# Where the seven-product partial sums are gathered, and how many blocks are dense, in a float32 transformer layer on one core

## The reference

```python
def swiglu(x, w_gate, w_up, w_down):
    return (jax.nn.silu(x @ w_gate) * (x @ w_up)) @ w_down

def reference(...):                      # DEPTH = 1, D_MODEL = 2048, FFN_DIM = 5632
    h = swiglu(rms_norm(x, ffn1_pre_g[l]), ffn1_w_gate[l], ffn1_w_up[l], ffn1_w_down[l])
    x = x + 0.5 * rms_norm(h, ffn1_post_g[l])
    ...                                  # attention part, untouched
    h = swiglu(rms_norm(x, ffn2_pre_g[l]), ffn2_w_gate[l], ffn2_w_up[l], ffn2_w_down[l])
    x = x + 0.5 * rms_norm(h, ffn2_post_g[l])
```

## Time and profile before

| | |
|---|---|
| time, median of 3 runs | 1757.99 us (1757.85 to 1758.72) |
| span of the profiled execution | 1756.5 us (the page has no separate time for it) |
| TensorE busy | 1737.1 us, 99% |
| VectorE busy | 1410.7 us, 80% |
| ScalarE busy | 1001.8 us, 57% |
| DMA | 389.75 MB, mean 222 GB/s |

### The profile page before, as it was taken

One profiled execution on the slowest core, in us unless ns is written; L12 is line 12 of the kernel. 1 busy time (PEld: TensorE's weight loads), 2 busy tenths in 40 slices (PEclk: granted clock), 3 DMA queues, 4 the chain that ended last, 5 costly groups with the idle time before them and its releaser, 6 DMA issues. The chain is left out here.

```text
span 1756.5 us, 21394 instructions
## 1 busy us (share of the span) xinstructions
PE 1737.1 (99%) x7968; PEld 1442.3 (82%) x7968; DVE 1410.7 (80%) x1284; ACT 1001.8 (57%) x979; POOL 65.3 (4%) x99
## 2 busy tenths in 40 slices
PE   9999999999999999999999999999999999999998
PEld 8788888888888888788888878788888888888886
DVE  7888888888888888765578558888888888888887
ACT  6666565555655654543347446555666666555563
POOL 1000000000000000010000000000000000000000
PEclk9999999999999999999999999999999999999999
DMA  9777777777766554355441546777777777666453
GB/s 386 237 257 259 256 256 239 239 239 248 245 234 222 184 215 176 147 219 189 174 162 54 187 171 260 263 240 241 249 249 241 239 246 251 254 232 238 174 191 114
DMA packets 58978, 389.75 MB, mean 222 GB/s; under 512 B 6432, under 2 KB 6688, under 8 KB 16160
## 3 DMA queue, kind: packets, MB, share of 16 engines
q1 hardware_dynamic: 52720, 344.77, 50.1%
q0 software_dynamic: 6048, 44.04, 13.2%
q10 hardware_dynamic: 144, 0.04, 0.0%
HBM read 384.63 MB, written 4.19 MB: 221 GB/s over the span
## 5 line engine op out<-in xcount | busy, mean ns | idle before, releaser
L2093 PE MATMUL banks<-w_hi,act_hi 128*128 128x512 f32 (+1 forms) x1088 | 424.7, 390 | 1.1 <-DVE act_lo L1355 1.1
L2095 PE MATMUL banks<-w_hi,act_lo 128*128 128x512 f32 (+1 forms) x1088 | 421.5, 387 | 0.0
L2094 PE MATMUL banks<-w_lo,act_hi 128*128 128x512 f32 (+1 forms) x1088 | 421.2, 387 | 0.0
L1385 DVE TENSOR_TENSOR op_lo<-quads,op_hi 128x2048 fp32r<-128x2048 f32 x140 | 318.5, 2288 | 43.2 <-ACT op_hi L918 42.8
L918 ACT ACTIVATE op_hi<-quads 128x2048 fp32r<-128x2048 f32 x140 | 266.8, 1919 | 53.3 <-PE banks L2095 21.1
L2287 PE MATMUL banks<-w_hi,hid_split 128*128 128x512 f32 x992 | 275.1, 389 | 0.5 <-DVE hid_split L1616 0.5
L1374 DVE TENSOR_TENSOR w_lo<-raw,w_hi 128x2048 fp32r<-128x2048 f32 x80 | 181.3, 2287 | 78.3 <-ACT w_hi L892 78.3
L1344 DVE TENSOR_TENSOR w_lo<-raw,w_hi 128x2048 fp32r<-128x2048 f32 (+3 forms) x67 | 143.8, 2147 | 121.6 <-ACT w_hi L843 121.6
L2093 PEld LDWEIGHTS banks<-w_hi,act_hi 128*128 128x128 f32 x1088 | 204.6, 188 | 42.1 <-issue 1.8
L2095 PEld LDWEIGHTS banks<-w_hi,act_lo 128*128 128x128 f32 x1088 | 204.4, 188 | 41.7
L2094 PEld LDWEIGHTS banks<-w_lo,act_hi 128*128 128x128 f32 x1088 | 204.6, 188 | 40.0
(11 more groups left out here) (209 smaller groups left out, 2329.8 us busy)
## 6 DMA issues: line engine op xcount, KB each, us to landing
raw<-in_weights SPq DMA_DIRECT2D x203, 1024.0 KB, 5.1
quads<-in_paired SPq DMA_DIRECT2D x80, 1024.0 KB, 10.7
quads<-in_paired POOLq DMA_DIRECT2D x40, 1024.0 KB, 8.5
raw<-in_paired SPq DMA_DIRECT2D x32, 768.0 KB, 5.9
rows<-in_x SPq DMA_DIRECT2D x4, 1024.0 KB, 10.9
raw<-in_weights SPq DMA_DIRECT2D x6, 512.0 KB, 3.5
gain_row<-in_post_gains SPq DMA_DIRECT2D x3, 1024.0 KB, 6.6
raw<-in_weights SPq DMA_DIRECT2D x4, 768.0 KB, 4.1
```

Source lines behind the costliest of these rows:

```text
L1385: nc.vector.tensor_tensor(op_lo[:, slot, :], op_raw(op), op_hi[slot][:, :], ALU.subtract)\
L2093: nc.tensor.matmul(out_ap, hi, rhs_hi, start=start, stop=False, skip_group_check=chain)
L2094: nc.tensor.matmul(out_ap, hi, rhs_lo, start=False, stop=False, skip_group_check=chain)
L2095: return nc.tensor.matmul(out_ap, lo, rhs_hi, start=False, stop=stop, skip_group_check=chain)
```

## The change

- `DENSE = 4`: blocks 0 to 3 are dense, so that nine units are left. Blocks 0 to 2 run ahead of the first unit. Block 3 runs inside it: its four pieces (`ahead`, B_0 to B_3) stand where a unit has plain pieces, and a unit's own plain pieces follow one unit later, except one. TensorE's order in a unit is P3, P1, L_A, P7, P6, turn, L_B, P2, L_C, P5, P4, turn, L_D. L_D holds near chunks of this unit; L_A (near), L_B and L_C (far) are those of the unit before. After the last unit L_A, L_B, L_C remain as a tail.
- The gathering moves into PSUM. ScalarE copies P3 and P7 to SBUF and P1 into the near block's bank, each times the inverse of the RMS factor (`inv`); VectorE begins the three other banks with `inv` times X plus or minus a kept part (`begin_bank`). The remaining products and the plain pieces then accumulate on these banks. SiLU and the product with the up half read them, with the RMS factor as scale. `join_part` and `mix_block` go.
- The near block's banks alternate (2, 3 and 6, 7); the far block's are 0, 1.
- P1's activations get their own scaled copy (`a11_hi`, `a11_lo`); `act_hi` keeps its values.
- The two accumulating DMAs are cut in rows of 1024 elements instead of 2048.
- The SP queue's loads follow the new order; the second unit's L_A waits for `piece_used` of B_3.
- In the down stage's start the order of the first pieces changes a little.

```diff
-UNITS = N_FB // 2
+DENSE = 4
+UNITS = (N_FB - DENSE) // 2
...
-            def join_part(part, t, other, op=ALU.add):
-                nc.vector.tensor_tensor(part[:, t, :], part[:, t, :], other, op).then_inc(parts_joined, 1)
-
-            def mix_block(stage, u, part, bank, behind, joined, sign=ALU.add):
...
+            def begin_bank(bank, t, negative, kept_part, op):
+                nc.vector.scalar_tensor_tensor(
+                    out=banks[:, bank, :], in0=banks[:, X_BANK, :], scalar=inv[:, negative, t:t + 1], in1=kept_part,
+                    op0=ALU.mult, op1=op).then_inc(banks_added, 1)
+            def begin_near(stage, v):
+                dve.wait_ge(part_kept, per_unit(stage, v.u, 3, 3))
+                dve.wait_ge(piece_used, used(stage, v, O_P6))
+                begin_bank(near_bank(v) + 1, 1, 0, kept7[:, :], ALU.add)
+            def begin_far(stage, v):
...
+                dve.wait_ge(piece_used, used(stage, v, O_P5))
+                begin_bank(FAR_BANK, 0, 1, kept3[:, :], ALU.add)
+                begin_bank(FAR_BANK + 1, 1, 1, kept7[:, :], ALU.subtract)
```

ScalarE's kept and begun parts, and its unit:

```diff
+            def keep_p3(stage, v):
...
+                nc.scalar.activation(kept3[:, :], banks[:, near_bank(v), :], ACT.Copy, scale=inv[:, 0, 0:1])\
+                  .then_inc(part_kept, 1)
+            def begin_near(stage, v):
...
+                nc.scalar.activation(banks[:, near_bank(v), :], banks[:, X_BANK, :], ACT.Copy, scale=inv[:, 0, 0:1])\
+                  .then_inc(part_kept, 1)
+            def keep_p7(stage, v):
...
+            def unit(stage, v, last=False):
+                keep_p3(stage, v)
+                operand_high(stage, v, O_P7)
+                begin_near(stage, v)
+                operand_high(stage, v, O_P6)
+                plain_high(stage, v, L_B)
+                gate_near(stage, before, v)
+                plain_high(stage, v, L_C)
+                keep_p7(stage, v)
+                operand_high(stage, v, O_P2)
                 operand_high(stage, v, O_P5)
+                keep_hidden(stage, near_block(before))
+                plain_high(stage, v, L_D)
                 operand_high(stage, v, O_P4)
+                gate_far(stage, before, v)
+                plain_high(stage, behind, L_A)
+                if not last:
+                    operand_high(stage, behind, O_P3, v)
+                    operand_high(stage, behind, O_P1, v)
+                keep_hidden(stage, far_block(before))
```

VectorE's unit:

```diff
             def unit(stage, v, last=False):
+                sum2(stage, v)
                 operand_low(stage, v, O_P7)
                 operand_low(stage, v, O_P6)
+                plain_low(stage, v, L_B)
+                multiply_hidden(stage, near_block(before), near_bank(before))
+                plain_low(stage, v, L_C)
                 operand_low(stage, v, O_P2)
+                begin_near(stage, v)
+                operand_low(stage, v, O_P5)
+                plain_low(stage, v, L_D)
                 operand_low(stage, v, O_P4)
+                multiply_hidden(stage, far_block(before), FAR_BANK)
+                plain_low(stage, behind, L_A)
+                begin_far(stage, v)
                 if not last:
+                    operand_low(stage, behind, O_P3)
+                    operand_low(stage, behind, O_P1)
+                    sum3(stage, behind)
```

TensorE's first unit, and from the SP and POOL queues the wait for B_3 and the size of an accumulating load's rows:

```diff
+            def first_unit(stage):
+                v = FIRST
                 product(stage, v, O_P3)
                 product(stage, v, O_P1)
+                turn_hidden(stage, 2)
+                ahead_product(stage, 0)
                 product(stage, v, O_P7)
                 product(stage, v, O_P6)
+                ahead_product(stage, 1)
+                product(stage, v, O_P2)
+                ahead_product(stage, 2)
                 product(stage, v, O_P5)
+                ahead_product(stage, 3)
+                product(stage, v, O_P4)
+                plain_product(stage, v, L_D, v)
...
+                    sp.wait_ge(piece_used, used(stage, v, B_3))
+                    load_plain(stage, behind, L_A)
...
                                     .rearrange("o p n -> (o p) n"), accum_op=ALU.add,
+                                    max_dma_last_dim=2 * OPERAND).then_inc(sum1_landed, 16)
```

More of the change, by code:

```diff
@@ L646, in load_units @@
[L646 to L651 removed]
+                sp.wait_ge(lo_ready, made(stage, LAST, L_B))
+                load_plain(stage, LAST, L_D)
+                sp.wait_ge(lo_ready, made(stage, LAST, L_C))
```

714 lines of the change are left out of this document (401 added, 313 removed).

## The result

The changed kernel takes 1761.84 us (median of 20 runs, 1759.69 to 1766.48), the kernel before, run beside it, 1758.68 us (20 runs, 1757.59 to 1759.95). The ratio is 1.0021, 95% interval [1.0014, 1.0027]: about 3 us and just over 0.2% slower, where I had forecast 1758.2 us and no difference. It lies inside the stated range (1756.0 to 1763.5) and 0.3 us above the 0.2% band. Its runs also spread more, 6.8 us against 2.4.

What follows compares the result with a forecast made beforehand. TensorE, busy 1737.1 of 1756.5 us, bounds the kernel. Span 1756.5 + 5.4 (products) - 6.0 (waits) + 0.8 (second unit's P1) = 1756.7, with 1.5 us over the span 1758.2 us; range 1756.0 to 1763.5.

Steps and rivals of the forecast that it cites:

- 0.2% band: Whole kernel: 0.2% or 3.5 us is about what a measurement can tell from no change, 1754.5 to 1761.5 us.
- the side that I had given 0.22: Whole kernel: slower than before by more than 0.2%, chance 0.22.
- other rivals: Range's upper end 1763.5: waits returning elsewhere (0.13), middle-unit cover used up (0.06), late second-unit L_A and P1 (0.18).
- 24 matmuls, +5.4 us: Gate/up stages: two dense blocks more, one unit less per network add 12 matmuls each, +5.4 us on TensorE.
- The waits of the old first units, -6.0 us: Start of both gate/up stages: TensorE's waits and late steps, 3.0 us per network, all go.
- Middle units unchanged: Middle gate/up units: they keep 41.77 us without TensorE waits; less helper work gives nothing there.
- P1 of the second unit, +0.8 us: Second unit: L_A, requested only when B_3 is used, makes P1 0.4 us late, twice; really late: chance 0.18.
- Second accumulating load: Each unit, ahead of P4: issued at 10.3, landed by 20 us; even with doubled landing in time, no cost.
- The down stage ... No change.: Start of the down stage: VectorE has the first piece ready 1 us before, so no added time.
- The clock: Idle time at 1044 to 1046 us: drop cost about 1.7 us; spared 1755.7, chance 0.06; striking twice 1759.9.
- the third: First units: old waits return at other places, half of the 6.0 us stay, 1761.2 us; chance 0.13.

Runs made afterwards that it cites:

- combined version: Changed kernel with accumulating loads in long rows, side sums moved before the last block's second plain piece, pauses filled with products of zeros: 1757.55 us, ratio 0.9992.
- room experiment: Changed kernel, short rows kept, with 1792 instead of 1024 bytes per partition set aside for GpSimd's transfer descriptions: 1760.42 us, ratio 1.0006.
- run with held loads: Changed kernel with SyncE's loads behind the second unit's near-block third piece held until that unit's second accumulating load has landed: 1768.93 us, ratio 1.0053.

## Where the prediction was right, and where it failed

The time lies inside the range, but 3.6 us above the forecast, on the side that I had given 0.22. The mechanism that I built the forecast on held: the added products and the removed waits nearly cancel, and nothing happens in the middle units. What made the kernel slower came from terms that I had put at nothing, the second accumulating load above all. The range had room for them only because I had widened it for other rivals; that the time fell inside it is in part luck.

Point by point, in the profiled executions:

- **24 matmuls, +5.4 us.** Right, shown alone by the run with 12 products more.
- **The waits of the old first units, -6.0 us.** Right in kind, too large. In the combined version the stages are 21.93 and 21.84 us shorter than in the earlier trace rows; a unit less and a dense block more inside them are 41.77 - 22.24 = 19.53. That leaves 2.40 and 2.31, less 0.15 each for its better start of the down stage, plus 0.3 each ahead of P3: 5.0 us. I had also counted as a wait the 0.38 us step at the end of the stage, which the change did not remove. The old waits differ by up to 1.3 us per network from one profile to another, so this term is no firmer than that.
- **Middle units unchanged.** Right, to 0.01 us, and 80 us less of VectorE gave nothing.
- **P1 of the second unit, +0.8 us.** About +0.2. The wait for B_3 was where I said (load at 114.72, forecast 114.6); L_A landed in 4.8 us instead of 5.1, and P1's step was 0.32 us.
- **Second accumulating load.** This is the step that failed most. I wrote that in a unit the loads are "issued at 2.7 and 10.3" and "if that doubled the landing, P4's remainder would come at 31 to 32, still before 33.1". In the second unit (P3 at 123.05) the remainder that the load waits for was made at 11.8, the load was begun at 14.6 and had landed at 30.3; with 1.92 and 2.29 us of splitting P4 could start at 34.6, against 33.5. Two things were missing: that the short rows could hold the second load until the first had landed, which the room experiment shows, and that a first unit needed its own sum, since its loads are bunched. Cost: steps 1.15 + 0.3 us longer in this profile, 1.8 us of the two stages with the slower restart, 3.4 in the one with the side sums moved; in the runs, with what follows from it, the step from 1.0021 to 1.0003.
- **"The down stage ... No change."** Wrong by 0.37 us twice. I had "its first piece ready 1 us before" TensorE. It was ready 0.5 us after TensorE wanted it (476.12 against 475.64). The four side sums had stood ahead of it before as well; new ahead of it is the operand's remainder, 1.7 us in the list, and without that the piece is ready 1.2 us before, about what I wrote. So that is the term I most likely left out. Moving the sums away removed the step too.
- **The clock.** I had priced a drop at 1.7 us; the kernel before's cost 0.7 and the changed kernel's 0.8 and 0.9. In this profile it did strike twice, as the rival had it: 1.1 us more than before. That need not be the change's doing: the five other versions of the changed kernel without filling each have one such stretch at these two places, and so has the kernel before.

The sum with what was measured: 1756.5 + 5.4 - 5.0 + 0.2 + 1.8 + 0.7 + 1.1 = 1760.7, the span being 1760.6. Without the second load's lateness it would have been 1759, and the run with long rows had 1757.7, with one clock drop fewer. Without the clock's term the sum is 3.1 us over the kernel before, close to the 3.2 us between the medians. Among the rivals, the third (waits that return at other places of the first units) was nearest in place and size.

## What to carry to other kernels

When a change lengthens one queue's work list (here twice the rows per transfer), work out the first and last units for themselves and not from the steady one: the steady unit had over 2 us of cover everywhere, the second had none. A diff's smallest edit, one argument of a transfer, was its dearest; try such arguments alone. And when an engine at 99% gains by removing waits what it loses by doing more products, only the waits that come new decide.

## What the runs showed of the hardware

- An accumulating load of 1 MB from GpSimd in rows of 4 KB makes 256 packets where one in rows of 8 KB makes 128, takes GpSimd 1.2 instead of 0.87 us to begin, and with 1024 bytes set aside per partition a second one wanted earlier was held until the first had landed (8.7 to 9.2 us after the first, against 6.7 to 6.8 in long rows, at the first or second units); with 1792 bytes it wasn't.
- Beside SyncE's transfers a second load landed after up to 15.7 us in short rows in the changed kernel's profile (17.1 at most in the other runs) and up to 12.2 with long rows (12.7 in the combined version), where the median was 10.8 and 9.4.
- TensorE's pauses of 1.0 and 1.7 us in one turning of the rows, and of 0.6 and 1.4 us in the other, were followed by a stretch at the lower clock in some profiled executions and not in others: of the ten kernels without filling the changed kernel had it at both places and each other one at one of them. With products of zeros in the pauses it stayed at the upper level in all three kernels that had them. Such a stretch cost 0.7 to 1.4 us there against the filled versions, and 2.0 in the run with held loads, where it was twice as long. Little of that, 0.3 us in the changed kernel's profile, came from the turns of 128 columns inside it.
